# Convolution taps split by chunk: two diagonal products and twelve side taps in chunks 0 to 5, thirteen diagonal products in chunk 7, whose input is formed within chunk 6

## What is computed

```python
u = h @ pw1_w + pw1_b                       # 1024 -> 2 x 1024
a, g = jnp.split(u, 2, axis=-1)
u = a * jax.nn.sigmoid(g)
# centred depthwise convolution over the tokens, 31 taps for each channel
u = lax.conv_general_dilated(u, dw_w[:, None, :], window_strides=(1,), padding=[(15, 15)],
                             dimension_numbers=('NWC', 'WIO', 'NWC'),
                             feature_group_count=u.shape[-1]) + dw_b
u = jax.nn.silu(layernorm(u, n_w, n_b))
return u @ pw2_w + pw2_b
```

## Time and profile before

| | us |
|---|---|
| median of three runs | 2202.14 |
| their range | 2197.51 to 2206.18 |
| the profiled execution | 2196.35 |
| its span, first to last instruction | 2194.6 |
| first pointwise product to last mean product, in the trace | 1212.4 to 1369.7 |
| mean granted clock of PE, share of 2.4 GHz | 0.939 |

### The profile page before, as it was taken

One profiled execution on the slowest core, in us unless ns is written; L12 is line 12 of the kernel. 1 busy time (PEld: TensorE's weight loads), 2 busy tenths in 40 slices (PEclk: granted clock), 3 DMA queues, 4 the chain that ended last, 5 costly groups with the idle time before them and its releaser, 6 DMA issues.

```text
span 2194.6 us, 30702 instructions
## 1 busy us (share of the span) xinstructions
PE 1838.0 (84%) x9312; PEld 952.4 (43%) x9313; DVE 878.0 (40%) x1540; ACT 464.1 (21%) x826; POOL 368.0 (17%) x556
## 2 busy tenths in 40 slices
PE   5989999888999888887981997879988899988942
PEld 3455555444444444444431442344544444444521
DVE  1555656455322222221216598574322222222235
ACT  4144444221111111010111454231111111110102
POOL 0010000001111111111105387001111111111122
PEclk9999999999999999999995998889999999999985
DMA  9497011256899999999979002264999999999954
GB/s 396 168 356 295 1 39 77 115 202 258 307 421 394 401 398 396 398 403 393 384 280 344 30 1 115 99 250 174 361 408 400 397 398 409 397 400 396 395 175 164
DMA packets 94960, 625.09 MB, mean 285 GB/s; under 512 B 16048, under 2 KB 16176, under 8 KB 56880
## 3 DMA queue, kind: packets, MB, share of 16 engines
q1 hardware_dynamic: 43920, 499.70, 56.9%
q0 software_dynamic: 26112, 79.72, 10.0%
q10 hardware_dynamic: 24864, 44.84, 5.7%
HBM read 563.38 MB, written 76.28 MB: 291 GB/s over the span
## 4 chain that ended last, share of the span: by engine, by line
PE 55%; DMA 21%; DVE 8%; issue 4%; POOL 3%; ACT 2%; DVEq 0%; ACTq 0%; SPq 0%; POOLq 0%
DMA ring<-in 19%; PE PS L1005 10%; PE PS L1011 9%; PE PS L1215 5%; PE PS L1032 5%; PE PS L1018 5%; PE PS L1043 3%; PE PS L1233 3%; PE PS L934 3%; PE PS L996 3%; POOL work L558 2%; PE PS L987 2%; PE PS L952 2%; PE PS L962 2%; DMA y_rows<-work 1%
## 5 line engine op out<-in xcount | busy, mean ns | idle before, releaser
L1011 PE MATMUL PS<-ring,work 128*64 128x256 f32 x3360 | 413.7, 402 | 112.9 <-issue 110.4
L1011 PEld LDWEIGHTS PS<-ring,work 128*64 128x64 f32 x3360 | 246.4, 144 | 256.0 <-issue 159.4
L1397 DVE TENSOR_TENSOR work<-work,PS 64x256 f32<-64x256 f32 x105 | 44.4, 423 | 522.5 <-ACT work L641 518.9
L1018 PE MATMUL PS<-ring,work 128*64 128x512 f32 x840 | 204.9, 609 | 3.1 <-ACT work L667 2.6
L1005 PE MATMUL PS<-ring,work 128*128 128x512 f32 x368 | 164.9, 601 | 15.5 <-issue 8.9
L510 POOL COPY col_i<-idx 128x1 int32 (+1 forms) x128 | 23.2, 181 | 841.3 <-PE PS L1043 827.3
L1402 DVE COPY work<-PS 128x1024 f32<-128x1024 f32 x128 | 156.8, 1225 | 12.4 <-PE PS L1043 2.2
L516 POOL DMA_INDIRECT work<-h_rows,col_i x128 | 124.8, 975 | 166.6 <-issue 166.6
L641 ACT ACTIVATE work<-PS 64x256 f32<-64x256 f32 x105 | 39.5, 376 | 482.2 <-PE PS L1011 480.0
L1043 PE MATMUL PS<-cst,work 128*128 128x128 f32 x1040 | 140.8, 278 | 0.0
L1043 PEld LDWEIGHTS PS<-cst,work 128*128 128x128 f32 x1040 | 113.3, 141 | 54.1 <-issue 53.7
(11 more groups left out here) (238 smaller groups left out, 2171.8 us busy)
## 6 DMA issues: line engine op xcount, KB each, us to landing
ring<-in SPq DMA_DIRECT2D x154, 2048.0 KB, 17.4
ring<-in SPq DMA_DIRECT2D x128, 1024.0 KB, 18.1
y_rows<-sq POOLq DMA_DIRECT2D x2, 14336.0 KB, 57.9
y_rows<-work ACTq DMA_DIRECT2D x210, 128.0 KB, 9.1
ring<-in SPq DMA_DIRECT2D x3, 4096.0 KB, 13.6
ring<-in SPq DMA_DIRECT2D x4, 3072.0 KB, 12.1
y_rows<-work ACTq DMA_DIRECT2D x46, 256.0 KB, 10.9
h_rows<-work ACTq DMA_DIRECT2D x8, 512.0 KB, 15.5
```

The source lines that it names most:

```text
L1011: last = mm(bank(6)[64 * q:64 * q + 64, 0:F], lhs(c)[:, 0:64], w13(s)[:, q, c, :], start=(c == 0), stop=(c == DC - 1), tile_position=(0, 6 ...
L1018: last = mm(bank(4)[64 * q:64 * q + 64, :], actT[par][:, kk, 0:64], w2(s)[:, kk, q * 512:(q + 1) * 512], start=(kk == 0), stop=(kk == 1), ...
```

## The change

The taps are no longer shared out alike in all chunks:

| chunk | VectorE | PE | side taps (ACT and POOL) |
|---|---|---|---|
| all, before | 17 | 3 | 11 |
| 0 to 5, after | 17 | 2 | 12 |
| 6, after | 17 | 3 | 11 |
| 7, after | 10 | 13 | 8 |

The 13 diagonals of chunk 7 have a place of their own and are formed by ACT ahead of the loop, so ACT's order changes there too; chunk 7's products go into bank 0 and no longer wait for chunk 6 to be finished. VectorE forms chunk 7's input within its taps of chunk 6, ahead of tap 8, where before it came after line 1609. The counts in the waits follow the new shares (left out here where only that changes).

```diff
-SIDE_TAPS = 11
-PE_TAPS = 3
-DVE_TAPS = TAPS - SIDE_TAPS - PE_TAPS
+SIDE_TAPS = (12,) * 6 + (11, 8)
+PE_TAPS = (2,) * 6 + (3, 13)
+DVE_TAPS = tuple(TAPS - a - b for a, b in zip(SIDE_TAPS, PE_TAPS))
...
-        diag = [[work[:, DG + (n * PE_TAPS + q) * 128:DG + (n * PE_TAPS + q + 1) * 128] for q in range(PE_TAPS)] for n in range(2)]
+        TAP_BANK = (7,) * (DC - 1) + (0,)
+        FEW = max(PE_TAPS[:-1])
+        DGL = DG + 2 * FEW * 128
+
+        def diag(c, q):
+            at = DGL + q * 128 if c == DC - 1 else DG + (c % 2 * FEW + q) * 128
+            return work[:, at:at + 128]
+
+        def sides(c):
+            return sum(SIDE_TAPS[:c])
+
+        def diags(c):
+            return PE_TAPS[-1] + sum(PE_TAPS[:c]) if c < DC else sum(PE_TAPS)
...
+            def diagonals(c):
+                for q in range(PE_TAPS[c]):
+                    at = c * TAPS + DVE_TAPS[c] + q
+                    A(diag(c, q), ident, ACT.Copy, scale=v("dww", at, at + 1)).then_inc(diag_rdy, 1)
+
+            diagonals(DC - 1)
             for c in range(DC):
                 if c:
-                    side_taps(c - 1, 0, SIDE_TAPS // 2)
+                    side_taps(c - 1, 0, SIDE_TAPS[c - 1] // 2)
...
-                if c >= 2:
-                    a.wait_ge(tap_ps, c - 1)
-                for q in range(PE_TAPS):
-                    at = c * TAPS + DVE_TAPS + q
-                    A(diag[c % 2][q], ident, ACT.Copy, scale=v("dww", at, at + 1)).then_inc(diag_rdy, 1)
+                if c < DC - 1:
+                    if c >= 2:
+                        a.wait_ge(tap_ps, c - 1)
+                    diagonals(c)
                 if c:
-                    side_taps(c - 1, SIDE_TAPS // 2, SIDE_TAPS)
+                    side_taps(c - 1, SIDE_TAPS[c - 1] // 2, SIDE_TAPS[c - 1])
...
             def conv_taps(c):
                 pe.wait_ge(u_rdy, c + 1)
-                pe.wait_ge(diag_rdy, PE_TAPS * (c + 1))
-                if c:
+                pe.wait_ge(diag_rdy, diags(c + 1))
+                if 0 < c < DC - 1:
                     pe.wait_ge(cv_rdy, c)
-                for q in range(PE_TAPS):
-                    last = mm(bank(7), diag[c % 2][q], up[c % 2][:, DVE_TAPS + q:DVE_TAPS + q + T], start=(q == 0), stop=(q == PE_TAPS - 1))
+                for q in range(PE_TAPS[c]):
+                    at = DVE_TAPS[c] + q
+                    last = mm(bank(TAP_BANK[c]), diag(c, q), up[c % 2][:, at:at + T], start=(q == 0), stop=(q == PE_TAPS[c] - 1))
                 last.then_inc(tap_ps, 1)
...
-                for q in range(2, DVE_TAPS - 2):
+                for q in range(2, DVE_TAPS[c] - 2):
+                    if c == DC - 2 and q == DVE_TAPS[c] // 2:
+                        glu_out(DC - 1)
                     link(V.scalar_tensor_tensor(sums[q % 2], up[c % 2][:, q:q + T], tap(q), sums[q % 2], ALU.mult, ALU.add), 1)
...
-                if c + 1 < DC:
+                if c + 2 < DC:
                     glu_out(c + 1)
                 dve.wait_ge(tap_ps, c + 1)
-                link(V.tensor_tensor(conv[:, c, :], conv[:, c, :], bank(7), ALU.add))
-                dve.wait_ge(side_add, (SIDE_TAPS - 1) * (c + 1))
+                link(V.tensor_tensor(conv[:, c, :], conv[:, c, :], bank(TAP_BANK[c]), ALU.add))
+                dve.wait_ge(side_add, sides(c + 1) - c - 1)
                 V.tensor_tensor(conv[:, c, :], conv[:, c, :], side[c % 2], ALU.add).then_inc(cv_rdy, 1)
```

More of the change, by code:

```diff
@@ L242, in build @@
         DG = CU + DC * T + 10 * T
[L243 to L244 removed]
+        TAP_BANK = (7,) * (DC - 1) + (0,)
[8 more added lines that the diff above has]
+            return PE_TAPS[-1] + sum(PE_TAPS[:c]) if c < DC else sum(PE_TAPS)
+        assert DGL + PE_TAPS[-1] * 128 <= 12800
         oF = conv
@@ L574, in _ @@
             for c in range(DC):
-                for q in range(1, SIDE_TAPS):
-                    n = c * SIDE_TAPS + q
+                for q in range(1, SIDE_TAPS[c]):
+                    n = sides(c) + q
                     pool.wait_ge(side_mul, n + 1)
@@ L796, in side_taps @@
                 for q in range(q0, q1):
-                    n = c * SIDE_TAPS + q
+                    n = sides(c) + q
                     if n >= 4:
-                        a.wait_ge(side_add, (n - 4) // SIDE_TAPS * (SIDE_TAPS - 1) + max(1, (n - 4) % SIDE_TAPS))
-                    at = TAPS - SIDE_TAPS + q
+                        d = c if q >= 4 else c - 1
+                        a.wait_ge(side_add, sides(d) - d + max(1, n - 4 - sides(d)))
+                    at = TAPS - SIDE_TAPS[c] + q
                     A(tap_prod[n % 4], up[c % 2][:, at:at + T], ACT.Copy, scale=v("dww", c * TAPS + at, c * TAPS + at + 1))\
                         .then_inc(side_mul, 1)
+            def diagonals(c):
[3 more added lines that the diff above has]
+            diagonals(DC - 1)
             for c in range(DC):
                 if c:
-                    side_taps(c - 1, 0, SIDE_TAPS // 2)
+                    side_taps(c - 1, 0, SIDE_TAPS[c - 1] // 2)
                 a.wait_ge(glu_ps, c + 1)
@@ L820, in _ @@
                     A(cs_row, cs_row, ACT.Silu).then_inc(crow_rdy, 1)
-            side_taps(DC - 1, 0, SIDE_TAPS)
+            side_taps(DC - 1, 0, SIDE_TAPS[DC - 1])
             a.wait_ge(cent_rdy, DC)
@@ L1590, in glu_out @@
                 if c >= 2:
-                    dve.wait_ge(side_mul, SIDE_TAPS * (c - 1))
+                    dve.wait_ge(side_mul, sides(c - 1))
                     dve.wait_ge(tap_ps, c - 1)
@@ L1603, in _ @@
                 link(V.tensor_scalar(sums[1], up[c % 2][:, 1:1 + T], tap(1), None, ALU.mult), 1)
-                for q in range(2, DVE_TAPS - 2):
+                for q in range(2, DVE_TAPS[c] - 2):
+                    if c == DC - 2 and q == DVE_TAPS[c] // 2:
+                        glu_out(DC - 1)
                     link(V.scalar_tensor_tensor(sums[q % 2], up[c % 2][:, q:q + T], tap(q), sums[q % 2], ALU.mult, ALU.add), 1)
-                for q in range(DVE_TAPS - 2, DVE_TAPS):
+                for q in range(DVE_TAPS[c] - 2, DVE_TAPS[c]):
                     link(V.scalar_tensor_tensor((conv[:, c, :], tmp[c % 2])[q % 2], up[c % 2][:, q:q + T], tap(q), sums[q % 2],
-                                                ALU.mult, ALU.add), 1 if q < DVE_TAPS - 1 else 0)
+                                                ALU.mult, ALU.add), 1 if q < DVE_TAPS[c] - 1 else 0)
                 link(V.tensor_tensor(conv[:, c, :], conv[:, c, :], tmp[c % 2], ALU.add))
-                if c + 1 < DC:
+                if c + 2 < DC:
                     glu_out(c + 1)
                 dve.wait_ge(tap_ps, c + 1)
-                link(V.tensor_tensor(conv[:, c, :], conv[:, c, :], bank(7), ALU.add))
-                dve.wait_ge(side_add, (SIDE_TAPS - 1) * (c + 1))
+                link(V.tensor_tensor(conv[:, c, :], conv[:, c, :], bank(TAP_BANK[c]), ALU.add))
+                dve.wait_ge(side_add, sides(c + 1) - c - 1)
                 V.tensor_tensor(conv[:, c, :], conv[:, c, :], side[c % 2], ALU.add).then_inc(cv_rdy, 1)
```

## The result

| | before | after |
|---|---|---|
| median, us | 2202.14 | 2192.16 |
| profiled execution, span | 2194.6 | 2182.9 |
| second sigmoid to first centring subtraction | 126.95 | 119.47 |

The medians are of seven executions of each kernel. The ratio of the first comparison is 0.9945, with a 95% interval from 0.9928 to 0.9961. The forecast, 2194.3, is a ratio of 0.9964 to the median it was made from. One execution of a later run, the kernel before with one operand from PSUM, took 3924.66 us, where its nine others took 2193.73 to 2202.37; it is left out of that run's ratio.

A forecast was written before the change was run, and what follows sets the result against it. TensorE's 16.3 us a chunk sets the pace in the second layer's convolution, VectorE and POOL close behind. Last sum 6.85 us earlier plus 0.95 on the last mean product, 7.8 us, takes 2202.14 to 2194.3; range 2188 to 2199.

The forecast's parts named there:

- The loop of VectorE and POOL: Chunks 0 to 5: chunk starts by turns 15.1 and 17.7 us apart; of 5.2 us PE is spared, 1.5 reach VectorE.
- The last sum: Chunk 7 on VectorE: done at 1360.9 against 1367.73, 6.85 us earlier.
- The hidden work: ACT: 13 diagonals, 3.8 us, fit its 10.56 us wait; chunk 7's sigmoid is ready with 2.4 us in hand.
- The loads behind the last pointwise product: SP's loads go out 4.6 us earlier, into an idle DMA; costed at nothing.
- The last mean product: End of the stage on PE: after 2.1 us idle, at the held clock, about 1.0 us instead of 1.95.
- The clock: PE ahead of chunk 7's taps: idle 3.0 us in place of 10.23, full clock taken as held, though not by much.
- rival C: PE's clock falls in the 3.0 us gap and stays low: 7.9 us slower, 2210.0; chance 0.04.
- the prediction's own list: Signs in the changed profile, among them PE idle some 3 us, then 26 rows of tap products at full clock.
- A: Chunks 0 to 5: VectorE and POOL stop colliding, PE's 15.46 us pace holds; gain 12.2 + 0.95, 2189.0; chance 0.14.
- the collisions: VectorE's lines 1609 and 1615 against POOL's adds: whoever is second waits, VectorE some 1.0 us, POOL 0.27.
- B: Both VectorE additions wait for POOL in every chunk, chunk 6 starts as now; gain 5.2 us, 2196.9; chance 0.12.

The follow-up runs named there:

- the second ratio: The unmodified changed kernel timed again against the kernel before: 0.9963, interval 0.9948 to 0.9978, median 2193.22 us.

## Why the prediction held, step by step

**The loop of VectorE and POOL.** Counted from the second sigmoid (1242.82 in the profile that the forecast was made from, 1241.40 now), chunk 1 was forecast at 12.0, chunk 2 at 27.1, chunk 3 at 44.8, chunk 6 at 92.6 and chunk 7 at 108.7. They came at 11.99, 27.10, 44.81, 92.71 and 108.88. The last sum was to be done at 118.1 and is at 118.2. The experiments with chunks 0 to 5 alone and with the PSUM operands show that this is so for the reason given.

**The hidden work.** The 13 diagonals took 3.89 us and left ACT 5.53 us of idle time ahead of the first sigmoid, of 10.56. Chunk 7's sigmoid starts at 1336.26 and its input at 1339.43, 2.5 us after the sigmoid's end (2.4 forecast), so the new wait costs nothing. ACT's timeline:

```profile
1216.96 3.89 ACT L821 ACTIVATE work<-cst,vec 128x128 f32<-128x128 f32 x13
...
1227.67 0.69 ACT L830 ACTIVATE work<-PS,vec 128x512 f32<-128x512 f32 x1 [5.53 <-PE PS L1235]
...
1241.40 0.69 ACT L830 ACTIVATE work<-PS,vec 128x512 f32<-128x512 f32 x1 [8.10 <-PE PS L1235]
...
1336.26 0.67 ACT L830 ACTIVATE work<-PS,vec 128x512 f32<-128x512 f32 x1
```

The loads behind the last pointwise product, also costed at nothing, begin between 1334 and 1336 here and between 1340 and 1342 before; the stretch after the stage shows no order by kernel.

**The last mean product.** Forecast at 1.0 us, measured 1.13. With VectorE's last sum it gives the centring at 119.47 after the second sigmoid; 119.1 was forecast. The idle ahead of it, forecast at 2.1 us, was 0.34 in the first profile and 2.04 in the second, and the product took 1.13 and 1.12.

**The clock, where a step failed.** After 3.0 us of idle I took the clock as held. PE stood 2.74 us, and in the first profile the clock fell (busy time by stretch; the granted clock is the third number from the end):

```profile
1340.00:1342.00 2.00, 1.77 (x4) 0.83 (x5) 2.00 (x4) 1.31 (x2) 1.86 (x2) 0.85 0.94 401
...
1342.00:1344.00 2.00, 2.00 (x4) 0.85 (x3) 2.00 (x4) 0.72 (x2) 1.86 (x2) 0.50 1.03 442
...
1344.00:1346.00 2.00, 2.00 (x5) 0.81 (x4) 2.00 (x4) 1.20 (x2) 1.71 (x3) 0.80 1.05 451
```

In the second profile of the same kernel, with 2.72 us of idle, it did not:

```profile
1340.00:1342.00 2.00, 0.39 (x1) 0.00 (x0) 2.00 (x4) 1.69 (x3) 1.81 (x2) 1.00 0.95 393
...
1342.00:1344.00 2.00, 0.88 (x2) 0.49 (x3) 2.00 (x4) 0.79 (x2) 1.86 (x2) 1.00 1.06 451
...
1344.00:1346.00 2.00, 2.00 (x6) 0.94 (x5) 2.00 (x4) 1.13 (x2) 1.71 (x3) 1.00 0.98 418
```

The 13 products took 12.96 us from their start to the mean's in the one (1340.23 to 1353.19), 11.26 in the other. The seven mean products end at 1359.36 there, 0.3 us ahead of the last sum's end, and at 1360.55 here, 2.0 us ahead. PE in the second profile:

```profile
1343.12 11.43 PE L1225 MATMUL PS<-work 128*128 128x512 f32 x26 [2.72 <-DVE work L1613]
...
1354.38 6.17 PE L1243 MATMUL PS<-work,mean_w 128*128 128x512 f32 x14
```

So the fall to 0.50, 1.2 GHz, costs 1.7 us (2.2 forecast in rival C), VectorE's longer chain hides it, as the forecast said, and the stage is 119.47 in both. But the cover is down to 0.3 us: the step that failed is the clock held through the idle ahead of chunk 7's taps, and it cost nothing only because VectorE ended later still. By the prediction's own list the 13 products were to run at the full clock; in one of two profiles they did.

**The rivals.** A needed the collisions to fall apart; they did not, and the run without them gives what A was worth: a stage of 114.15, 12.8 us less than before (13.2 in the forecast; the ratio measured is 0.9923). Part of the 12.8 is not the change's, since the same edit gave the kernel before 2.6. B, a wait in both lines in every chunk, did not come about: line 1631's late input is what lets line 1637 pass. C was a clock that stays low; in the run with the input where it was, after 9.49 us of idle, the clock was back at full by 1366, within the 13 products that run from 1358.71 to 1372.89.

**The measurement.** By the first ratio, 0.9945, the gain is half a per cent and not the 0.35 of the forecast; the second, 0.9963, is near it. The intervals of the two overlap, from 0.9948 to 0.9961, so by the runs alone they need not differ. The forecast had no term for the stretches outside the stage, which made 4.2 of the 11.7 us in the first pair of profiles; what moves them is open. That the second ratio comes so near the forecast is in part chance: the stage gave 0.3 us less than forecast, and the interval is 6.6 us wide.

## What to carry to other kernels

Work taken off the busiest engine is worth what the next loop of engines allows: here TensorE was spared 5.2 us in six chunks, and the loop of VectorE and GpSimd, which took 16.4 us a chunk where TensorE would have allowed 15.5, let 0.8 to 1.7 of it through. Write out the loop chunk by chunk with the trace's own start-to-start times, collisions included, before giving a second engine more work. Where additions on VectorE run beside GpSimd, try first to leave one operand in PSUM: here that cost no instruction and gave 5.3 us on the changed kernel and 2.6 on the one before.

## What the runs showed of the hardware that was not expected

The granted clock fell in one execution and not in another after the same idle of 2.7 us with the same work before it, so an idle of this length can go either way; the shortest idle at which the forecast had seen it fall was 3.40 us.

The collisions were in the forecast; the runs give their size and their limit. An addition of VectorE with two SBUF operands that comes second waits up to 1.04 us for a GpSimd addition. The one that comes first stretches a GpSimd addition from 1.27 to as much as 1.64 in the changed kernel, and to 1.67 in the run with chunks 0 to 5 alone. With one operand in PSUM neither happens (0.69 and 1.28 at most). The Trainium skill, in "SBUF — State Buffer", section "Who interferes with whom", says that a VectorE instruction with two SBUF inputs contends with a GpSimd one that reads SBUF, and that one with at most one SBUF input, outside the two-port modes, does not; the runs agree with both. The prediction drew from there that the first to start holds the port for its whole length. By the stretched adds it is less: VectorE's addition kept GpSimd's off for some 0.55 of its 0.69 us, in the kernel before (from 1348.30, the add at 1348.57 stretched by 0.28) and in the changed one (from 1279.86, the add at 1280.05 stretched by 0.36).
